# A chunked delta-rule inversion in a one-core hybrid block: T set up by transposing U for both heads, one mask of U on GpSimd, and the rows of four delta heads read two stages earlier

## The reference

```python
decay = jnp.exp(jnp.where(incl, gc[..., :, None] - gc[..., None, :], -jnp.inf))
A = jnp.where(strict, jnp.einsum('bhnld,bhnmd->bhnlm', k, k) * decay * beta[..., :, None], 0.0)
sol = lax.linalg.triangular_solve(A + jnp.eye(L, dtype=A.dtype), rhs, left_side=True, lower=True, unit_diagonal=True)
u, w = sol[..., :Dv], sol[..., Dv:]
attn = jnp.einsum('bhnld,bhnmd->bhnlm', q, k) * decay
```

## Time and profile before

| what | us |
| --- | --- |
| median of three executions | 2211.17 |
| the profiled execution | 2211.99 |
| its span, first to last instruction | 2210.2 |
| mean granted TensorE clock | 0.992 |
| TensorE busy (matmul) in the span | 2137.8 (97%) |
| VectorE busy | 1291.0 (58%) |
| ScalarE busy | 907.7 (41%) |
| GpSimd busy | 119.1 (5%) |

### The profile page before, as it was taken

How to read it: one execution, slowest core, us unless ns; L and a number is a source line. 1 busy time by engine, 2 the same in 40 slices (tenths; PEclk the granted TensorE clock), 3 DMA queues, 4 the chain that set the end, 5 groups by cost and what they waited for, 6 DMA issues and landing times. The chain is left out here.

```text
span 2210.2 us, 35946 instructions
## 1 busy us (share of the span) xinstructions
PE 2137.8 (97%) x14174; PEld 1705.1 (77%) x14174; DVE 1291.0 (58%) x1739; ACT 907.7 (41%) x1421; POOL 119.1 (5%) x96
## 2 busy tenths in 40 slices
PE   8999999999999999999999999999887899999999
PEld 6787788888877777778888887678776566888887
DVE  6564576663378877566665347687466566333333
ACT  4444532222365666552222234655232544323221
POOL 0000011110000000001111000000233000000000
PEclk9999999999999999999999999999999999999999
DMA  7331233333324221223333331323000112333331
GB/s 256 105 114 59 76 115 95 95 97 102 96 69 141 84 74 47 96 67 114 95 95 104 95 95 58 94 81 91 3 4 4 47 39 67 105 97 103 95 95 66
DMA packets 54087, 189.77 MB, mean 86 GB/s; under 512 B 5968, under 2 KB 6224, under 8 KB 53840
## 3 DMA queue, kind: packets, MB, share of 16 engines
q1 hardware_dynamic: 53680, 187.49, 27.8%
q10 hardware_dynamic: 288, 0.59, 0.1%
HBM read 184.91 MB, written 3.15 MB: 85 GB/s over the span
## 5 line engine op out<-in xcount | busy, mean ns | idle before, releaser
L299 PE MATMUL l_banks<-l_r_hi,l_w_hi 128*128 128x512 f32 x1440 | 574.6, 399 | 4.4 <-DVE l_r_lo L1796 2.4
L301 PE MATMUL l_banks<-l_r_hi,l_w_lo 128*128 128x512 f32 x1440 | 561.7, 390 | 0.0
L300 PE MATMUL l_banks<-l_r_lo,l_w_hi 128*128 128x512 f32 x1440 | 561.4, 390 | 0.0
L284 DVE TENSOR_TENSOR l_w_lo<-ring,l_w_hi 128x1024 fp32r<-128x1024 f32 x216 | 299.0, 1386 | 96.7 <-ACT l_w_hi L278 93.1
L278 ACT ACTIVATE l_w_hi<-ring 128x1024 fp32r<-128x1024 f32 x216 | 227.2, 1056 | 291.5 <-PE l_banks L301 286.7
L299 PEld LDWEIGHTS l_banks<-l_r_hi,l_w_hi 128*128 128x128 f32 x1440 | 270.7, 188 | 73.1 <-issue 8.3
L300 PEld LDWEIGHTS l_banks<-l_r_lo,l_w_hi 128*128 128x128 f32 x1440 | 270.9, 188 | 57.8 <-issue 4.3
L301 PEld LDWEIGHTS l_banks<-l_r_hi,l_w_lo 128*128 128x128 f32 x1440 | 270.6, 188 | 57.1
L299 PE MATMUL ff_banks<-ff_r_hi,ff_w_hi 128*128 128x512 f32 x512 | 200.0, 391 | 0.0
L301 PE MATMUL ff_banks<-ff_r_hi,ff_w_lo 128*128 128x512 f32 x512 | 199.2, 389 | 0.0
L300 PE MATMUL ff_banks<-ff_r_lo,ff_w_hi 128*128 128x512 f32 x512 | 199.2, 389 | 0.0
(11 more groups left out here) (516 smaller groups left out, 3221.9 us busy)
## 6 DMA issues: line engine op xcount, KB each, us to landing
ring<-weights SPq DMA_DIRECT2D x315, 512.0 KB, 3.6
na_bias<-window_bias SPq DMA_DIRECT2D x16, 512.0 KB, 5.6
da_rel<-t_rel SPq DMA_DIRECT2D x8, 448.0 KB, 4.2
outT<-X SPq DMA_DIRECT2D x12, 256.0 KB, 2.1
X<-xT SPq DMA_DIRECT2D x8, 256.0 KB, 5.6
const<-consts SPq DMA_DIRECT2D x1, 1312.0 KB, 11.4
l_pt<-pT SPq DMA_DIRECT2D x2, 512.0 KB, 4.6
X<-outT SPq DMA_DIRECT2D x4, 256.0 KB, 3.6
```

The lines of the kernel that those rows point to most:

```text
L284: dve.tensor_tensor(self.w_lo[:, c % self.slots, :], k.ring[:, g % RING, :], self.w_hi[:, c % self.slots, :].bitcast(F32), ALU.subtract).t ...
L299: pe.matmul(psum, hi, self.hi(rhs_slot), start=start, stop=False)
L300: pe.matmul(psum, hi, self.lo(rhs_slot), start=False, stop=False)
L301: return pe.matmul(psum, lo, self.hi(rhs_slot), start=False, stop=stop)
```

## The change

1. **T from U.** `init` keeps only the subtraction for U. `turn_u` transposes both heads' halves of U (16 matmuls, in the four-quadrant order of `invert_x`, into the banks of `finish_wu`), and stands two places earlier, in level 4 of the stage before, between `invert_x` and `invert_p`. Its result is copied to T by ScalarE in one instruction of 128 x 512, behind level 4's `xt_out`. `finish_wu` also waits for that copy.
2. **The mask of U.** For delta pairs GpSimd multiplies `dect` with `up0` into U, between the two decay masks; the second of them waits for it, since it writes over `dect`. VectorE's `ar_out` multiplies the products with it into U, and the other half of the products with `dect` into `ar`: four instructions of 128 x 256 in place of two of 128 x 512.
3. **Rows.** The rows of pairs 4 and 5 (four heads) are read in level 3 (keys) and level 4 (queries) of stages 2 and 3. Pair 3's stay where they were. Banks and waits are set to fit.

The diff, cut to its core (the changed waits on `dmask` and `t_init` are counters only):

```diff
@@ bank, key_bank
+            if i == MIX_T + 1 and n < 2:
+                n -= 2
...
-            return SETUP[((18, 29, 40)[i] + n) % 3]
+            return SETUP[((18, 29, 42)[i] + n) % 3]
@@ TensorE
-                def setup_rows(i):
+                def setup_rows(i, part):
                     bb = k.c("pair_sel", slice(64, 70))[:, (i - MIX_T) * P:(i - MIX_T + 1) * P]
...
+                    if part == 0:
+                        pe.wait_ge(s["x1_out"], MIX_T) if i == MIX_T else pe.wait_ge(s["a_out"], 2 * i)
                     else:
...
+                        pe.wait_ge(s["key_out"], 3) if i == MIX_T else pe.wait_ge(s["ar_out"], 2 * i - 1)
+                    pe.matmul(ps[:, bank(i, part), :], bb, rows[1 + part][64:70, :], start=True, stop=True).then_inc(s["bb_done"], 1)
...
+                    pe.wait_ge(s["t_init"], min(i + 2, PAIRS))
                     for t in range(TT):
...
                 def turn_u(i):
 
                     pe.wait_ge(s["u_init"], i + 1)
-                    if i:
-                        pe.wait_ge(s["t_out"], 4 * i)
-                    for u in range(TT, U8):
-                        for c in range(2):
-                            mm = pe.matmul(compact(P_B)[half(1 - c), u, :], U[i % 2][half(c), u, :], k.c("ident2", half(c)), start=True, stop=True)
+                    if i >= 2:
+                        pe.wait_ge(s["yn_out"], 2 * (i - 1))
+                    for t in range(TT):
+                        for pair in DIAG:
+                            for c, h in pair:
+                                mm = pe.matmul(ps[half(c ^ h), F0 + h, t * CHUNK:(t + 1) * CHUNK], U[i % 2][half(c), TT * h + t, :], k.c("ident2", half(c)),
+                                               start=True, stop=True)
                     mm.then_inc(s["turned_u"], 1)
...
+                turn_u(0)
                 for i in range(PAIRS):
                     nxt = i + 1 < PAIRS
-                    turn_u(i)
...
-                    if nxt and delta(i + 1):
-                        setup_rows(i + 1)
+                    if i + 1 == MIX_T:
+                        setup_rows(MIX_T, 0)
+                        setup_rows(MIX_T, 1)
...
                     invert_x(i, 3)
...
+                    if MIX_T < i + 2 < PAIRS:
+                        setup_rows(i + 2, 0)
                     invert_p(i, 3)
                     invert_x(i, 4)
...
+                    if MIX_T < i + 2 < PAIRS:
+                        setup_rows(i + 2, 1)
+                    if nxt:
+                        turn_u(i + 1)
                     invert_p(i, 4)
@@ ScalarE
+                def turned_out(i):
+                    act.wait_ge(s["turned_u"], i + 1)
...
+                    act.activation(by_head(T[i % 2]), ps[:, F0:F1 + 1, 0:HALF], ACT.Copy).then_inc(s["t_init"], 1)
...
                     xt_out(i, 4)
                     if nxt and not delta(i + 1):
                         x1(i + 1)
+                    if nxt:
+                        turned_out(i + 1)
@@ GpSimd, decay_masks
                     pool.tensor_tensor(dec[:, :, :], dec[:, :, :], over(k.c("strict_low")), ALU.mult).then_inc(s["dmask"], 1)
+                    pool.wait_ge(s["wu_ps"], i - 1)
+                    pool.wait_ge(s["turned_u"], i - 1)
+                    pool.tensor_tensor(U[i % 2], dect[:, :, :], over(k.c("up0")[:, 0:CHUNK]), ALU.mult).then_inc(s["dmask"], 1)
+                    pool.wait_ge(s["dmask"], 3 * (i - MIX_T) + 2)
                     pool.tensor_tensor(dect[:, :, :], dect[:, :, :], over(k.c("incl_up")), ALU.mult).then_inc(s["dmask"], 1)
@@ VectorE, ar_out
-                            dve.tensor_tensor(ar[:, i % 2, c, :, :], units(bank(i, 7 + h)).rearrange("p t (k l) -> p t k l", k=2),
-                                              dect[:, c, :].unsqueeze(2).broadcast_to([P, TT, 2, CHUNK]), ALU.mult).then_inc(s["ar_out"], 1)
+                            dve.tensor_tensor(U[i % 2][:, c, :], units(bank(i, 7 + h))[:, :, 0:CHUNK], U[i % 2][:, c, :], ALU.mult).then_inc(s["chain"], 1)
+                            dve.tensor_tensor(ar[:, i % 2, c, 1, :], units(bank(i, 7 + h))[:, :, CHUNK:P], dect[:, c, :], ALU.mult).then_inc(s["ar_out"], 1)
@@ VectorE, init
-                    dve.tensor_tensor(t0, A[i % 2][:, 0:TT, :], over(level(0), TT), ALU.mult).then_inc(s["chain"], 1)
...
-                        dve.tensor_tensor(U[i % 2], ar[:, i % 2, :, 0, :], over(k.c("up0")[:, 0:CHUNK]), ALU.mult).then_inc(s["chain"], 1)
...
-                    dve.tensor_tensor(t0, over(k.c("ident2"), TT), t0, ALU.subtract).then_inc(s["t_init"], 1)
...
                     dve.tensor_tensor(U[i % 2], over(k.c("ident2")), U[i % 2] if delta(i) else ar[:, i % 2, :, 0, :], ALU.subtract).then_inc(s["u_init"], 1)
@@ VectorE, the loop
-                    turned_out(i)
...
-                    if nxt and delta(i + 1):
-                        delta_rows(i + 1)
+                    if i + 1 == MIX_T:
+                        key_rows(MIX_T)
+                        query_rows(MIX_T)
...
                     if nxt:
                         init(i + 1)
+                    if MIX_T < i + 2 < PAIRS:
+                        key_rows(i + 2)
                     update(i, 4)
+                    if MIX_T < i + 2 < PAIRS:
+                        query_rows(i + 2)
```

More of the change, by code:

```diff
@@ L2430, in by_keys @@
                     return mm
-                def setup_rows(i):
+                def setup_rows(i, part):
                     bb = k.c("pair_sel", slice(64, 70))[:, (i - MIX_T) * P:(i - MIX_T + 1) * P]
-                    if i == MIX_T:
-                        pe.wait_ge(s["x1_out"], MIX_T)
-                    elif i == MIX_T + 1:
-                        pe.wait_ge(s["ar_out"], 2 * MIX_T + 2)
-                    else:
-                        pe.wait_ge(s["a_out"], 2 * i)
-                    pe.matmul(ps[:, bank(i, 0), :], bb, rows[1][64:70, :], start=True, stop=True).then_inc(s["bb_done"], 1)
-                    if i < MIX_T + 2:
-                        pe.wait_ge(s["key_out"], (3, 5)[i - MIX_T])
-                    else:
-                        pe.wait_ge(s["ar_out"], 2 * i - 1)
-                    pe.matmul(ps[:, bank(i, 1), :], bb, rows[2][64:70, :], start=True, stop=True).then_inc(s["bb_done"], 1)
+                    if part == 0:
+                        pe.wait_ge(s["x1_out"], MIX_T) if i == MIX_T else pe.wait_ge(s["a_out"], 2 * i)
+                    else:
+                        pe.wait_ge(s["key_out"], 3) if i == MIX_T else pe.wait_ge(s["ar_out"], 2 * i - 1)
+                    pe.matmul(ps[:, bank(i, part), :], bb, rows[1 + part][64:70, :], start=True, stop=True).then_inc(s["bb_done"], 1)
                 def setup_tokens(i):
@@ L2450, in setup_tokens @@
                         at = 2 * (i - MIX_T)
-                        if i < MIX_T + 2:
-                            pe.wait_ge(s["key_out"], (4, 6)[i - MIX_T])
+                        if i == MIX_T:
+                            pe.wait_ge(s["key_out"], 4)
+                        elif i == MIX_T + 1:
+                            pe.wait_ge(s["rows_out"], 4)
                         else:
@@ L2531, in setup_keys @@
                     else:
-                        pe.wait_ge(s["a_out"], 2 * (i + 1) + 2)
+                        pe.wait_ge(s["ar_out"], 2 * (i + 1) + 2)
                     turn(lambda t: keys(i)[:, t * P:t * P + P], key_bank(i, 0), "keys_turned")
@@ L2535, in setup_keys @@
                     if i == 2:
-                        pe.wait_ge(s["ar_out"], 2 * (i + 1) + 1)
+                        pe.wait_ge(s["kb_out"], 2)
                     turn(lambda t: ki[:, i, t * P:t * P + P], key_bank(i, 1), "keys_turned")
@@ L2743, in _ @@
                 tokens(0)
+                turned_out(0)
                 for i in range(PAIRS):
@@ L2828, in delta_rows, with query_rows @@
                     dve.tensor_tensor(kr[:, n, :, 0, :], tiles(keys(i)), tiles(ps[:, bank(i, 0), :]), ALU.mult).then_inc(s["kb_out"], 1)
+                def query_rows(i):
+                    n = i - MIX_T
                     dve.wait_ge(s["bb_done"], 2 * n + 2)
@@ L2922, in update @@
                         dve.wait_ge(s["p_ps"], 4 * i + lv + 1)
-                        dve.wait_ge(s["t_out"], 4 * i + lv) if lv else dve.wait_ge(s["t_init"], 2 * i + 2)
+                        dve.wait_ge(s["t_out"], 4 * i + lv) if lv else dve.wait_ge(s["t_init"], i + 1)
                         dve.tensor_tensor(T[i % 2], T[i % 2], compact(P_B), ALU.subtract).then_inc(s["t_out"], 1)
```

30 lines of the change are left out of this document (13 added, 17 removed).

## The result

The changed kernel takes 2217.08 us (median of 13 executions, 2211.78 to 2223.0) against 2210.53 of the kernel before, measured beside it (13, 2207.31 to 2214.95): a ratio of 1.0025, 95% interval 1.0016 to 1.0034, that is 5.5 us more. Kernels that were measured side by side are a *batch*, with executions of the kernel before of its own. In a second batch it was 1.0028 (1.0018 to 1.0038). The forecast was 2.3 us less. It lies outside the range, and the change is slower by more than the 0.2% that can be told from nothing.

The account below looks back on a forecast made before the run. The operator stage was taken as a chain passing between engines, none of them full. Joins -4.7, rows -1.7 and +0.1, mask +4.0 gave -2.3 us, a median of 2208.9 us; range 2204.6 to 2213.4.

Parts of the forecast that it names:

- Part 1, the joins: Five joins between stages and the stage's start: U's shorter path on VectorE and the earlier turn give 4.7 us less.
- The lower bound of 2.5: Least gain at the joins, if the turn cost twice 0.65 instead of 0.52 and half the first join were lost.
- Part 2, the rows: Rows moved out of levels 0 to 1: 0.86 us less in each of stages 3 and 4, together 1.7 less.
- "0.07 too much": Level 3: a row between its first two products takes 1.48 us where 1.41 lie; twice, 0.1 us more.
- Rival D: The rows' move costs in levels 3 and 4 what it gives in 0 and 1; -0.6 us, chance 0.10.
- Part 3, the mask: U's mask between GpSimd's decay masks delays level 3 in stages 2, 3 and 4; 4.0 us more in all.
- "The forecast leaves the falls as many as they are": Clock in the operator stage: idle time filled at joins and made at level 3, so falls, 1.60 us each, stay as many.
- Rival B: Clock falls behind the longer level-3 waits, three new falls of 1.60 us; net +2.5 us, chance 0.12.
- "The change fills idle time at the joins": Joins between stages: TensorE's idle time there is filled, set against the new idle time at level 3.
- Rival C: GpSimd's mask holds up VectorE's subtraction for U by 1.26 us in five joins; net +4.0 us, chance 0.06.
- Rival A: With the joins' idle time filled the clock stays at 2.4 GHz, two falls less, 3.2 us; net -5.5, chance 0.20.

Follow-up runs that it names:

- c2: e7 with the rows of pairs 4 and 5 back between levels 0 and 1; ratios 0.9969 and 0.9968 to the kernel before (-6.3 and -6.5 us).
- e5: Changed kernel with U's mask back on VectorE and the rows back, leaving only T from U; ratio 1.0026 to the kernel before (+5.3 us).
- e7: e2 with level 3's mask ahead of the decay masks on GpSimd; ratios 0.9977 and 0.9987 to the kernel before (-5.0 and -3.1 us).
- e2: Changed kernel with U's mask moved behind level 3's mask on GpSimd; ratio 0.9993 to the kernel before (-2.0 us).
- e3: Changed kernel with two products without a reader ahead of level 3's first product in stages 2 to 4; ratio 1.0003 to the kernel before (+0.7 us).
- p3: Changed kernel with 32 products without a reader, going round the places, at the stage's start; ratio 1.0018 to the kernel before (+4.0 us).
- p1: Kernel before with 16 products without a reader ahead of U's turn in each of six stages; ratio 0.9983 to the kernel before (-3.9 us).
- c1: p1 with level 3's mask ahead of the decay masks on GpSimd; ratio 0.9987 to the kernel before (-3.2 us).
- e4: Changed kernel with the rows of pairs 4 and 5 back between levels 0 and 1; ratios 1.0006 and 1.0011 to the kernel before (+1.2 and +3.0 us).
- p2: Changed kernel with 64 products without a reader, eight in a row per place, at the stage's start; ratio 1.0066 to the kernel before (+14.3 us).

## Why the prediction was wrong

- **Part 1, the joins: right.** 3.52 us where it said 3.5, the turn at 0.52, U's subtraction at 0.69. In c2's second trace, whose joins have neither fall nor break, the five sum to 17.6 against 22.3 before (its break of 1.18 left out): 4.7 less, where 4.3 was forecast for them. The lower bound of 2.5 doesn't follow from its own terms, since 0.78 more for the turn in five joins is 3.9; nothing hung on it. What the text missed is a condition: e5 shows that without part 3 the delta joins are longer than before.
- **Part 2, the rows: right at the place it looked at, wrong as a term.** L2564 (now L2566) to `finish_yn` is 2.15. But "0.07 too much" for a row in level 3 was 0.27 in the change's stage 3 (3.28 from L2606 to L2606, against 3.01 before) and 0.28 and 0.47 in e7; the lengths of products alone did not show it. With the rows put back the rest is 1.6 to 2.0 us lower (1.5 either way), not 1.6 higher. Rival D (the rows gain nothing) was nearer, with a chance of 0.10.
- **Part 3, the mask: right in size.** The waits grew by 4.4 and the path by 4.0 (7.11, 7.09 and 7.11 against 5.75, 5.76 and 5.77), as forecast. e2 gives back 4.6.
- **"The forecast leaves the falls as many as they are": wrong.** This is the first step that failed. The text had the row that speaks against it, a fall right behind 1.67 idle us, and had itself made three idle times of 1.7 to 2.1 (2.09 measured) out of shorter ones. It set them against the filled joins as an even exchange, without a count. In the traces the falls behind such waits came in 15 of 18, and the mean clock went from 0.9934 to 0.9904. Rival B named it, at 3 x 1.60; by the line the clock's part is 3.6 us in the second batch (2.5 to 4.3 by other slopes), and filling the three waits (e3) takes 4.6 away. B's number alone (+2.5) is still 3 short.
- **The breaks: not in the text.** "The change fills idle time at the joins" was read as gain only. 3.9 us in the trace became 8.6; p3 shows that some 3 us of time go with them. Three rows of the kernel before, with "issue" in the bracket in the middle of a group, would have told that TensorE is not always fed.
- **Rival C: rightly set aside** for the change; it is what e5 shows. **Rival A: wrong for the change, but its mechanism is real:** p1 fills the joins and nothing else, and gets an estimated 3.4 us by the clock, about the 3.2 that A gave.

The miss in numbers: forecast -2.3, measured +6.5 by the means of the second batch (+5.5 in the first). 3.6 of the 8.8 are the clock. For the other 5.2 there are some 3 of breaks, and 3.2 to 3.6 by which the rows cost instead of giving 1.6. These come to more than 6: each has an error of over 1, they were measured in different kernels and may in part be the same time, which the runs don't take apart.

## What to carry to other kernels

A wait that a sum of durations prices at its length costs more when TensorE is the one that waits: price the clock behind it as well, and try a few products without a reader in it before rebuilding the order. Where small products follow each other closely, look for waits inside a group, which no semaphore explains, and shift the program (p3: 32 products, some 128 instructions with their loads) before believing that an edit was slow for its own reasons. Two edits that free the same engine's slot (here T from U, and U's mask off VectorE) are tested together and apart, since one alone may turn the order of two contending instructions.

## What the runs showed of the hardware

- Products that compute nothing made the kernel before 3.9 us faster (p1); the granted clock was 0.9951 on average against 0.9922, which is 3.4 us by the line.
- Behind waits of 1.9 to 2.1 us ahead of level 3 the granted clock fell in 15 of 18 cases in six traces; behind waits of at most 0.76 or filled ones in none of 36.
- 0.001 of mean clock goes with about 1.2 us in this kernel (0.8 to 1.5 in the sets of ten or more executions, but c1's), that is 0.27 us for each us at half clock. At one place, in the join of stages 4 and 5, it was 1.60 for one low stretch.
- TensorE breaks off at places of its instruction stream that stand 127 to 134 records of products apart, each with its load. A break lasts up to 2.2 us, at the same place often the same to 0.01 (1.48 in e2, e4, p2). Most such places show no break in a given kernel. What decides which do was not found; 64 records more near the stage's start took most of them away (8.6 and 9.5 us to 2.8 in the change, 7.8 and 9.7 to 3.8 in c2).
- 64 products written eight at a time to the same place took 10.15 us, most of it at the lower clock (p2); the 16 of p1, two at a time and at full clock, took 1.15.
